# Head sums of four query or key tiles in one array pass, one inversion for four, and the inverted roots copied to the heads' partitions by transfers

## The reference, cut to what matters

```python
def rmsnorm(x, g):
    x32 = x.astype(jnp.float32)
    y = x32 * lax.rsqrt(jnp.mean(x32 * x32, axis=-1, keepdims=True) + EPS)
    return (y * g.astype(jnp.float32)).astype(x.dtype)

def q_heads(p_q, qg, n_heads, n_kv, rope):
    B, n, _ = p_q.shape
    q = rmsnorm(p_q.reshape(B, n, n_heads, HEAD_DIM), qg)      # HEAD_DIM = 64
    if rope is not None:
        q = apply_rope(q, *rope)
    return q.reshape(B, n, n_kv, n_heads // n_kv, HEAD_DIM)
```

## Time and profile before

| | us |
|---|---|
| median of 3 runs | 3042.7 |
| lowest, highest | 3042.65, 3042.92 |
| the profiled execution | 3041.93 |
| its span (first to last instruction) | 3039.8 |
| PE busy in the span | 2926.5 |
| DVE busy | 1115.6 |
| ACT busy | 622.8 |

### The profile page before, as it was taken

The page is one execution under the profiler, slowest core; times in us unless marked ns, Lnnn a source line. Parts: engine busy times, 40 slices in busy tenths (PEclk is TensorE's granted clock), DMA queues, the critical chain, the costliest instruction groups (busy, mean ns, idle before and its releaser), DMA issues.

```text
span 3039.8 us, 33448 instructions
## 1 busy us (share of the span) xinstructions
PE 2926.5 (96%) x13265; PEld 1464.3 (48%) x13265; DVE 1115.6 (37%) x1678; ACT 622.8 (20%) x1157; POOL 78.3 (3%) x92
## 2 busy tenths in 40 slices
PE   7999999999999999999999999999979998999999
PEld 4565655555555222222234655677433333334547
DVE  4764546566614000000147554334121110138352
ACT  3145530000002110101022453111011101021161
POOL 1000000000000001102000000000000000000000
PEclk9999999999999999999999999999989999999999
DMA  8230013443523899999971201223489999974300
GB/s 256 66 94 15 15 38 129 174 165 125 165 78 111 355 374 396 368 401 349 364 208 38 80 28 30 74 83 90 180 337 417 418 418 418 418 227 114 83 1 28
DMA packets 252321, 587.50 MB, mean 193 GB/s; under 512 B 64280, under 2 KB 143912, under 8 KB 231048
## 3 DMA queue, kind: packets, MB, share of 16 engines
q1 hardware_dynamic: 237072, 554.02, 49.4%
q0 software_dynamic: 7680, 22.62, 2.5%
q10 hardware_dynamic: 7416, 8.71, 1.2%
HBM read 561.44 MB, written 15.21 MB: 190 GB/s over the span
## 4 chain that ended last, share of the span: by engine, by line
PE 87%; DMA 7%; DVE 3%; issue 1%; ACT 1%; SPq 1%; ACTq 0%; DVEq 0%; POOL 0%; POOLq 0%
PE ps L1076 26%; PE ps L1527 10%; PE ps L1651 7%; PE ps L1539 5%; PE ps L1141 5%; PE ps L1096 5%; PE ps L1191 5%; PE ps L1367 3%; PE ps L1355 3%; PE ps L1401 3%; PE ps L1204 2%; PE ps L1588 2%; PE ps L1165 2%; DMA ring<-in_w_e_up 1%; DMA ring<-in_w_e_down 1%; PE ps L1341 1%
## 5 line engine op out<-in xcount | busy, mean ns | idle before, releaser
L1076 PE MATMUL ps<-hT,ring 128*128 128x512 f32 (+1 forms) x1696 | 604.5, 514 | 3.5 <-ACT hT L1889 3.4
L1076 PEld LDWEIGHTS ps<-hT,ring 128*128 128x128 f32 x1696 | 321.9, 191 | 276.0 <-issue 251.9
L1527 PE MATMUL ps<-ring,hT 128*64 128x512 f32 x992 | 235.9, 605 | 3.0 <-DMA ring<-in_w_e_up 3.0
L1141 PE MATMUL ps<-hT,ring 128*128 128x512 f32 (+1 forms) x448 | 181.5, 533 | 0.7 <-DVEq L1874 0.7
L1651 PE MATMUL ps<-ring,hT 128*64 128x512 f32 x640 | 157.6, 602 | 17.4 <-DMA ring<-in_w_e_down 10.0
L1889 ACT ACTIVATE prob<-prob,nms 128x768 f32<-128x768 f32 (+5 forms) x224 | 159.2, 711 | 14.9 <-DVE nms L2582 4.5
L1191 PE MATMUL ps<-merged,ring 128*128 128x512 f32 (+1 forms) x384 | 142.7, 526 | 3.1 <-issue 3.1
L1367 PE MATMUL ps<-con,prob 128*128 128x128 f32 x872 | 140.1, 283 | 3.5 <-DVE merged L2606 1.6
L1076 PE MATMUL ps<-obuf,ring 128*128 128x512 f32 (+1 forms) x384 | 142.1, 523 | 0.0
L1367 PEld LDWEIGHTS ps<-con,prob 128*128 128x128 f32 x872 | 96.4, 140 | 91.8 <-issue 78.8
L1889 ACT ACTIVATE prob<-ps 128x768 f32<-128x768 f32 (+2 forms) x55 | 36.7, 667 | 490.7 <-PE ps L1076 418.9
(11 more groups left out here) (368 smaller groups left out, 3675.1 us busy)
## 6 DMA issues: line engine op xcount, KB each, us to landing
ring<-in_w_e_gate SPq DMA_DIRECT2D x79, 1024.0 KB, 15.4
ring<-in_w_e_up SPq DMA_DIRECT2D x65, 1024.0 KB, 14.4
ring<-in_w_e_down SPq DMA_DIRECT2D x60, 1024.0 KB, 13.5
ring<-in_w_in SPq DMA_DIRECT2D x49, 1024.0 KB, 6.1
ring<-in_w_ada SPq DMA_DIRECT2D x48, 1024.0 KB, 6.7
merged<-in_w_e_up SPq DMA_DIRECT2D x25, 1024.0 KB, 14.8
merged<-in_w_e_down SPq DMA_DIRECT2D x19, 1024.0 KB, 12.6
merged<-in_w_e_gate SPq DMA_DIRECT2D x18, 1024.0 KB, 16.0
```

Of the source, the lines that this page charges most:

```text
L1076: mm = pe.matmul(ps[:, b + a:b + e], lhs[:, k, :], rhs[:, k, a:e], start=k == 0, stop=k == nk - 1)
L1141: mm = pe.matmul(ps[:, BANK[SIDE]:BANK[SIDE] + hi - lo], ring3(slot)[:, k, m % 2 * P:(m % 2 + 1) * P], h3[:, k, lo:hi], start=k == 0, stop ...
L1527: mm = pe.matmul(ps[e * CX:(e + 1) * CX, b + h * 512:b + (h + 1) * 512], lhs, second_weights(slot_of[sub], e, h), start=k == 0, stop=k == ...
```

## The change

The tiles of a layer are taken in groups of four ("quads", in the order of their projections; the last has the rest: 4, 4, 2 tiles in layers 0 and 1, and 4, 4, 4, 1 in layer 2). One `hs` now does a quad: the squares of four tiles (four buffers, the four rows of `prob`) are multiplied by 32 columns of the matrix of ones, 16 of each head, and each tile's sums go to 32 rows of the same PSUM bank, with `tile_position=(0, 32 * r)`. One root and one inversion then serve four tiles. A new job `spread` issues two transfers a tile, one a head: a single row of inverse roots, read 64 times over, goes to the head's 64 partitions. New jobs `nrm` (gain and inverse root, one a tile) follow, and one `swap` for the quad, in which neighbouring tiles share a transfer. The buffers of spread roots and of turn terms lie in `merged` (layers 0 and 1) and `obuf` (layer 2).

```diff
-        roots = [rs, pr[:, 1, :]]
-        squares = [sq, pr[:, 2, :]]
-        turn_terms = [[b.rearrange("p (c f) -> p c f", c=2) for b in (pr[:, 0, 0:NX], merged[:, 4 * NT:4 * NT + NX])]] * 2
-        turn_terms.append([pr[:, 0, 0:NX].rearrange("p (c f) -> p c f", c=2), pr[:, 0:2, NX:NT]])
+        roots = [rs, sq]
+        squares = [pr[:, r, :] for r in range(4)]
+        by_tile = merged[:].rearrange("p (r t) -> p r t", t=NT)
+        inverse_roots = [by_tile[:, 0:4, :]] * 2 + [obuf[:, 0:4 * NX].rearrange("p (r t) -> p r t", t=NX)]
+        turn_terms = [by_tile[:, 4:8, 0:NX]] * 2 + [obuf[:, 4 * NX:8 * NX].rearrange("p (r t) -> p r t", t=NX)]
...
+            tiles = [j[1:] for j in jobs if j[0] == "qk"]
+            order, waiting, made = [], [], 0
             for j in jobs:
                 order.append(j)
-                if swaps:
-                    order.append(("swap",) + swaps.pop(0))
-                while len(rots) > 1:
-                    order.append(rots.pop(0))
-                if sums:
-                    t = sums.pop(0)
-                    order.append(("hs",) + t)
-                    rots.append(("rot",) + t)
-                    swaps.append(t)
-                if j[0] == "qk":
-                    sums.append(j[1:])
-            order += [("swap",) + t for t in swaps] + rots
-            for t in sums:
-                order += [("hs",) + t, ("swap",) + t, ("rot",) + t]
-            return order
+                for stages in waiting:
+                    order += stages.pop(0)
+                waiting = [stages for stages in waiting if stages]
+                if j[0] != "qk":
+                    continue
+                made += 1
+                if made % 4 == 0 or made == len(tiles):
+                    n = (made - 1) // 4
+                    quad = tiles[4 * n:made]
+                    sums = [("hs", l, n), ("spread", l, n)]
+                    normed = [("nrm",) + t for t in quad] + [("swap", l, n)]
+                    rots = [("rot",) + t for t in quad]
+                    if made == len(tiles) and l < 2:
+                        for stages in waiting:
+                            order += sum(stages, [])
+                        waiting = [[sums + normed]]
+                        late = rots
+                    else:
+                        waiting.append([sums, normed, rots])
+            assert not waiting
+            return order + late if l < 2 else order
...
-            attention, last = attention_order(l), first.pop()
-            assert last == last_rot(l, 1)
-            attention.insert(attention.index(("S", l, 1)) + 1, last)
+            attention, first, last = attention_order(l), first[:-2], first[-2:]
+            assert last[1] == last_rot(l, 1)
+            at = attention.index(("S", l, 1)) + 1
+            attention[at:at] = last
...
-        qn_ready = event("head_normed", of("hs"))
+        inverted = event("head_roots_inverted", of("hs"))
+        qn_ready = event("head_normed", of("nrm"))
         q_ready = event("head_rotated", of("rot"))
-        s_swapped = [sem(f"head_halves_swapped{n}") for n in range(2)]
-        rots = of("rot")
-        rot_number = {j[1:]: n for n, j in enumerate(rots)}
+        s_spread = sem("head_roots_spread")
+        s_swapped = sem("head_halves_swapped")
...
-                    need(qsq_ready, ("qk",) + j[1:])
+                    need(qsq_ready, ("qk",) + quads[j][-1])
                     b = begin(j, HEAD_SUMS)
-                    for a, e in halves(width(*j[1:])):
-                        mm = pe.matmul(ps[:, b + a:b + e], con[:, C_HEAD:C_HEAD + P], squares[hs_number[j] % 2][:, a:e],
-                                       start=True, stop=True)
+                    for a, e in halves(NT):
+                        for r, t in enumerate(quads[j]):
+                            if width(*t) >= e:
+                                mm = pe.matmul(ps[32 * r:32 * (r + 1), b + a:b + e], con[:, C_HEAD + HD - 16:C_HEAD + HD + 16],
+                                               squares[r][:, a:e], start=True, stop=True, tile_position=(0, 32 * r))
                     part(mm, j)
...
-                    n = hs_number[("hs",) + j[1:]]
+                    n = hs_number[quad_of[j[1:]]]
                     b = A.read(j)
-                    if n >= 2:
-                        A.read(hs_of[l][n - 2])
+                    if n >= 1:
...
-                    A.do(func(squares[n % 2][:, 0:w], qk_dest(*j[1:])[:, 0:w] if j in RAW else ps[:, b:b + w], ACT.Square), qsq_ready, j)
+                    A.do(func(squares[place_of[j[1:]]][:, 0:w], qk_dest(*j[1:])[:, 0:w] if j in RAW else ps[:, b:b + w], ACT.Square), qsq_ready, j)
                 elif kind == "swap":
-                    n = rot_number[j[1:]]
-                    A.need(qn_ready, ("hs",) + j[1:])
-                    if n >= 2:
-                        A.need(q_ready, rots[n - 2])
-                    t = qk_dest(*j[1:])[:, 0:NX].rearrange("p (c f) -> p c f", c=2)
-                    for r in range(0, P, HD // 2):
-                        to, at = slice(r, r + HD // 2), r + HD // 2 if r % HD == 0 else r - HD // 2
-                        act.dma_start(turn_terms[l][n % 2][to], t[at:at + HD // 2]).then_inc(s_swapped[n % 2], 16)
+                    quad = ("hs",) + j[1:]
+                    A.need(qn_ready, ("nrm",) + quads[quad][-1])
+                    if before_quad[quad]:
+                        A.need(q_ready, ("rot",) + quads[before_quad[quad]][-1])
+                    for a, e in kinds(quad):
+                        tiles = tiles_from(*quads[quad][a], e - a)
+                        for r in range(0, P, HD // 2):
+                            to, at = slice(r, r + HD // 2), r + HD // 2 if r % HD == 0 else r - HD // 2
+                            act.dma_start(turn_terms[l][to, a:e, :], tiles[at:at + HD // 2]).then_inc(s_swapped, 16)
+                elif kind == "spread":
+                    quad = ("hs",) + j[1:]
+                    A.need(inverted, quad)
+                    col = NT if hs_number[quad] % 2 == 0 else 0
+                    for r, t in enumerate(quads[quad]):
+                        w = width(*t)
+                        for h in range(2):
+                            root_row = bass.AP(sqrs, (32 * r + 16 * h) * 2 * NT + col, [[2 * NT, 1], [0, HD], [1, w]])
+                            act.dma_start(inverse_roots[l][h * HD:(h + 1) * HD, r, 0:w], root_row).then_inc(s_spread, 16)
                 elif kind == "hs":
                     n = hs_number[j]
-                    if n >= 2:
-                        A.need(qn_ready, hs_of[l][n - 2])
-                    elif n == 0:
+                    if n == 0:
                         A.need(*last_rs[0])
-                    root(roots[n % 2], j, width(*j[1:]), HD)
+                    b = A.read(j)
+                    parts = summed(j)
+                    for r, a, e in parts:
+                        ins = func(roots[n % 2][r, a:e], ps[r, b + a:b + e], ACT.Sqrt, bias=epsn[r, 0:1])
+                        if a == parts[-1][1]:
+                            A.do(ins, rms_ready, j)
+                        else:
+                            A.do(ins)
+                    A.release(j)
...
-                    root = roots[hs_number[j] % 2]
-                    V.do(v.reciprocal(root[:, 0:w], root[:, 0:w]))
+                    root, parts = roots[hs_number[j] % 2], summed(j)
+                    for r, a, e in parts:
+                        ins = v.reciprocal(root[r, a:e], root[r, a:e])
+                        if a == parts[-1][1]:
+                            V.do(ins, inverted, j)
+                        else:
+                            V.do(ins)
+                elif kind == "nrm":
+                    dve.wait_ge(s_spread, spread_at[quad_of[j[1:]]])
                     t = qk_dest(*j[1:])[:, 0:w]
-                    V.do(v.scalar_tensor_tensor(t, t, gain_col(*j[1:]), root[:, 0:w], ALU.mult, ALU.mult), qn_ready, j)
+                    V.do(v.scalar_tensor_tensor(t, t, gain_col(*j[1:]), inverse_roots[l][:, place_of[j[1:]], 0:w], ALU.mult, ALU.mult),
+                         qn_ready, j)
...
+                    t = qk_dest(*j[1:])[:, 0:NX]
+                    turn_term = turn_terms[l][:, place_of[j[1:]], :]
...
-                    V.do(v.tensor_tensor(t, t, halved(con[:, C_COS:C_COS + NX]), ALU.mult))
+                    dve.wait_ge(s_swapped, swap_at[quad_of[j[1:]]])
+                    V.do(v.tensor_tensor(turn_term, turn_term, con[:, C_SIN:C_SIN + NX], ALU.mult))
+                    V.do(v.tensor_tensor(t, t, con[:, C_COS:C_COS + NX], ALU.mult))
                     V.do(v.tensor_tensor(t, t, turn_term, ALU.add), q_ready, j)
```

More of the change, by code:

```diff
@@ L937, in width, with summed @@
             return NT if l == 0 or (l == 1 and name in ("ka", "kb")) else NX
+        def summed(quad):
+            wide = [r for r, t in enumerate(quads[quad]) if width(*t) == NT]
```

(10 more changed lines are left out.)

35 lines of the change are left out of this document (26 added, 9 removed).

## The result

The change makes the kernel slower: 3238.3 us (median of 4 runs) against 3042.7, a ratio of 1.0641 with a 95 % interval of 1.0628 to 1.0654. The forecast was 3284.

The account below looks back on a forecast made before the run. PE was taken as the bound, busy 2926.5 of 3039.8 us. Stalls less the 21.9 us saving add 218 us and clock 23, giving a 3281 us span and a 3284 us forecast; range 3050 to 3425.

Parts of the forecast that it names:

- What PE saves: Head sums on PE, four tiles side by side: freed of 8.4, 6.1 and 7.4 us by layer, together 21.9 us.
- Term 1, the pace of a spread: Spread transfers: one source row limits them to 26 to 52 GB/s; middle 39, 5.0 us wide, 3.35 narrow.
- One of my signs of being wrong: ACT's issue of a many-row transfer costing much more than 0.61 us, which would make ACT the limit.
- Term 2, the chains: PE waits where quad chains end late: layers 0, 1 and 2 at +90, +76 and +52, together +218 us.
- Clock: Granted clock falls behind eight long PE stalls, 2.9 us lost each: 23 us.
- Behind the first scores: Start of attention: maximum, exponential and first transposition come 6.0 us behind the first scores, as today.
- The rival with fast landings: Spreads land 2.0 us after issue, only the chain's length costs: 3064 us; chance 0.26.
- the 67 - 51 of the prediction: Layer 0, before the first scores, with fast landings: PE stands 16 us.
- The rival on the other side: Faster: saving kept if the last quad's chain ends before the second values' sums; 3035.5 us, full saving 3021; chance 0.08.

Follow-up runs that it names:

- no_spread_copy_first: no_spread with ACT's copy of the second values ahead of the last group's swap (norms still wrong): 3039.4 us, ratio 0.9985.
- regrouped: one_transfer with the copy first, groups of 4, 2, 4 and in layer 2 1, 4, 4, 4, last group's jobs between attention's first: 3073.4 us.
- sixteen_rows: Changed kernel, each spread reading the 16 partitions that hold the root 4 times each, not one 64 times: 3097.3 us, ratio 1.0171.
- neighbours_32_apart: Changed kernel with a quad's one-partition transfers reordered to partitions 0, 32, 16, 48, 64, 96, 80, 112: 3317.9 us (one run).
- copy_first: one_transfer with ACT's copy of the second values ahead of the last group's swap in layers 0 and 1: 3079.5 us, ratio 1.0115.
- no_spread: Changed kernel without the spread transfers; norms use the inverse roots as they lie, so results are wrong: 3051.3 us, ratio 1.0024.
- one_transfer: Changed kernel with one spread transfer a tile, from its 32 partitions, 4 times each, in place of two: 3096.5 us, ratio 1.0172.
- four_neighbours: Changed kernel, each spread reading 4 neighbouring partitions 16 times each: 3297.2 us (one run).

## Why the prediction was right, point by point

*What PE saves.* 21.9 us. Right: the sums are busy 20.6 us less, part of them at the low clock, and in no_spread_copy_first the first scores of the three layers come 9.5, 5.5 and 7.5 us early (forecast 8.4, 6.1 and 7.4), and 7.2 us of it remain in layer 2 of regrouped, with real transfers.

*Term 1, the pace of a spread.* The mechanism was right and shown by sixteen_rows and neighbours_32_apart. The size was 39 GB/s, the middle of two ends that no row favoured; the trace has 1.57 MB in 34.6 us, 45 GB/s, because after some 8 us the pace was that of two nearly throughout. That 39 came so near is luck within a range that was worked out. What I did not foresee is that the queue is full behind two such transfers, so that ACT itself stands in the issue (25.84 us for eight, not 4.9). One of my signs of being wrong, an issue much dearer than 0.61 us, was thus there to see. But sixteen_rows needs 8.1 us for the same eight issues, so the issue is long because the transfers ahead of it are slow, and not of itself. For the same reason a transfer landed 6.3 to 15.1 us after its own issue, and not up to 40 as I had said. In the forecast most of a spread's time was a landing, in which ACT makes one more square. Now ACT was held by the issues and the square came late: it is what the standing of 4.28 us (by a slot) and of 18.89 us (at the third sum) goes back to. The end of the stage hardly moved by it, since what it waits for is the chain through the landing.

*Term 2, the chains.* First to second sum of layer 0: forecast 22 us of standing, measured 4.28 + 8.33 = 12.6. Second sum to the first scores: 77 in one piece, measured 18.89 + 50.49 = 69.4 in two, since the third sum already waits for the square behind the second spread's issues, a place that I had not listed. Layer by layer the forecast of +90, +76, +52 stands against 78.6, 61.0 and 48.2, in which the clock is contained. Over the three layers I had PE standing 241 us (99, 83, 59) and it stood 185 (82, 61, 42). Much of the excess is the pace: the three spreads of layer 0 took 34.6, 34.5 and 20.4 us for 42, 42 and 22, which is 16 of its 17 us. That ACT's copy behind the swap ends last is shown by copy_first.

*Clock.* The sign was right, the size too low: 23 us forecast, 33.4 measured as the same work on PE taking longer. Fifteen stalls of more than 2 us fell into the three stages, not eight. The price of 2.9 us held where a stretch was read (no_spread); over all of them it is 33.4 / 15 = 2.2 at most. The length of the stall does not set it: behind the longest, 50.49 us, the granted clock was 0.50 for 4 us and 0.96 in the next 4, which lost 2.2 us.

*Behind the first scores.* I took the time from the first scores to the first transposition as unchanged. It was 1.0 us longer. Then PE stood 2.82 us at a transposition, for a copy that DVE does behind two late turns, with the low clock once more behind it. These are parts of the 7.6 and 5.8 us in the table; the rest is not taken apart. That is the step which was missing.

*How the sum came out near.* Idle time was forecast at 239 us more and was 187, the clock at 23 and was 33, the saving at 21.9 and was 20.6. The first is 52 us too high and the others 12 too low, and so the span was 41 us below the forecast. Part of the nearness is that these two misses have opposite signs.

*The rival with fast landings* (3064 us) was tested by sixteen_rows: 3097.3. It was 33 us too low, and the table shows where. The first scores of layer 0 stood 25.97 us and not 16 (the 67 - 51 of the prediction isn't worked out term by term, and so which term was short stays open), and in layer 1 22.63 and not 20. Landings took 3.0 to 4.6 us where ACT's queue alone moved data, and 6.6 at the last group of layer 0, where weights moved too, and not 2.0; layer 2 didn't keep its 7.4 us but lost 7.7, by waits of 4.05 us at a sum and 6.22 at a slot; and 12 us were lost behind the first scores.

*The rival on the other side.* Its deciding point, the copy ahead of the end of the second values, was named rightly: with it (and without transfers) the full saving arrives. It did not say that DVE's backlog of the last group then stands in attention, which takes it back.

What stays open: what fills the queue (in one_transfer, with 128 rows a transfer, the first two issues again took 0.7 and 0.6 us and the third 2.5, so the rows alone don't decide it), why the first two transfers of a quad don't overlap, and why four_neighbours was slower than the changed kernel.

## What to carry to other kernels

A row that was read 64 times over from one partition moved at 25 to 29 GB/s here, with nearly all of the 16 engines at it: read it from as many partitions as hold it, and let neighbouring transfers in a queue start 16 and not 32 partitions apart. Batching four items through one step saves that step's work, but everything behind them comes four at a time; before counting the gain, find who waits behind the batch, and place the batches where nothing urgent follows (here layer 2, behind long projections) rather than right ahead of a stage with two buffers. And a stall on PE costs more than its length, here some 2 to 3 us of clock each.

## What the runs showed of the hardware

- One source partition: 25 to 29 GB/s; two 16 or 64 apart: 53 in the mean of 26 us, 41 to 65 in its parts; two 32 apart: 26 and 27 in the stretch where two 16 apart moved 65 and 62; sixteen neighbours for each of two transfers: 179 GB/s.
- Of eight transfers of 64 rows out of one partition the first two issues took 0.6 us each, the third 4.3 and the fourth 6.0, and ACT did nothing else meanwhile.
- With an outer count of 4 in the source, the share of busy DMA engines fell from 0.94 to 0.23.
- Transfers of roots (128 and 192 KB) from sixteen partitions landed after 3.0 to 4.6 us where nothing else moved, and after 6.6 us beside weights; a swap of 64 KB takes 2.0.
- In the 4 us behind a stall of 4.28 us the granted clock was 0.61, and behind one of 50.49 us 0.50 and then 0.96: 1.6 and 2.2 us lost.
